# Denser steps of gated linear attention beside the last four projection tiles, the latents' scaling moved next to the last one, and five vector operations moved to GpSimd

## What is computed

```python
cq, ckv, kr, gq, gk, gv, gr, gg = jnp.split(x @ w_in, idx, axis=-1)
q = (rms_norm(cq, q_norm) @ w_uq).reshape(B, T, MLA_HEADS, MLA_NOPE + MLA_ROPE)
q_rope = apply_rope(q_rope, cos[:, None, :], sin[:, None, :])
k_rope = apply_rope(kr, cos, sin)
ckv = rms_norm(ckv, kv_norm)
...
o = o_intra + jnp.einsum('bhnid,bhndv->bhniv', q_t, S_prev)      # GLA, chunk by chunk
...
gla = rms_norm(gla_o.astype(dtype), gla_norm) * jax.nn.silu(gg.reshape(B, T, GLA_HEADS, GLA_DV))
mix = jnp.concatenate([mla, gla.reshape(B, T, GLA_WIDTH)], -1) @ w_out
```

## Time and profile before

| what | value |
|---|---|
| time of three runs, median | 1333.73 us (1331.41 to 1333.77) |
| the profiled execution's own time | 1331.96 us |
| its span in the trace | 1328.6 us |
| TensorE busy | 1248.8 us (94% of the span) |
| VectorE, ScalarE, GpSimd busy | 835.9, 561.2, 174.1 us |
| tiles 14 to 17 with slots 0 to 47, in the trace | about 240.4 to 342.0 us |
| end of that to the first attention scores | 342.0 to 397.4 us |

### The profile page before, as it was taken

How to read it: one execution, slowest core, us unless ns; L and a number is a source line. 1 busy time by engine, 2 the same in 40 slices (tenths; PEclk the granted TensorE clock), 3 DMA queues, 4 the chain that set the end, 5 groups by cost and what they waited for, 6 DMA issues and landing times. The chain is left out here.

```text
span 1328.6 us, 24499 instructions
## 1 busy us (share of the span) xinstructions
PE 1248.8 (94%) x9650; PEld 1179.7 (89%) x9650; DVE 835.9 (63%) x1324; ACT 561.2 (42%) x925; POOL 174.1 (13%) x217
## 2 busy tenths in 40 slices
PE   7999998999788997999999999999999999999896
PEld 7987777899667776899999999999999999999896
DVE  4122212344797776567897777777657666668877
ACT  4212223144644445543755445444473333333335
POOL 3524333110000000032100000000000000000752
PEclk9999999999899999999999999999999999999898
DMA  8749888333420012232336878768588555555003
GB/s 292 232 147 297 282 273 289 114 108 95 127 50 11 11 49 63 88 133 69 90 110 231 285 264 296 265 258 289 196 300 290 174 177 177 189 191 183 9 17 112
DMA packets 116536, 226.91 MB, mean 171 GB/s; under 512 B 13203, under 2 KB 60581, under 8 KB 114118
## 3 DMA queue, kind: packets, MB, share of 16 engines
q1 hardware_dynamic: 110278, 208.57, 46.1%
q0 software_dynamic: 6144, 16.79, 4.1%
HBM read 165.54 MB, written 58.73 MB: 169 GB/s over the span
## 5 line engine op out<-in xcount | busy, mean ns | idle before, releaser
L2775 PE MATMUL psum<-step_hid_hi,step_w_hi 128*128 128x258 f32 x784 | 160.3, 286 | 7.2 <-DVE y_sums L2826 3.6
L2775 PE MATMUL psum<-step_hid_hi,step_w_lo 128*128 128x258 f32 x784 | 159.2, 285 | 0.0
L2775 PE MATMUL psum<-step_hid_lo,step_w_hi 128*128 128x258 f32 x784 | 158.7, 284 | 0.0
L355 PE MATMUL psum<-xTh,win_hi 128*128 128x344 f32 (+1 forms) x432 | 148.2, 343 | 9.6 <-DVE xTl L408 9.5
L355 PE MATMUL psum<-xTh,win_lo 128*128 128x344 f32 (+1 forms) x432 | 139.8, 324 | 0.0
L355 PE MATMUL psum<-xTl,win_hi 128*128 128x344 f32 (+1 forms) x432 | 139.7, 323 | 0.0
L2775 PEld LDWEIGHTS psum<-step_hid_hi,step_w_hi 128*128 128x128 f32 x784 | 123.8, 193 | 7.7 <-issue 3.8
L2775 PEld LDWEIGHTS psum<-step_hid_hi,step_w_lo 128*128 128x128 f32 x784 | 122.8, 192 | 0.0
L2775 PEld LDWEIGHTS psum<-step_hid_lo,step_w_hi 128*128 128x128 f32 x784 | 122.5, 192 | 0.0
L2392 PE MATMUL psum<-x_t_hi,w_variant_hi 128*128 128x258 f32 x512 | 103.9, 284 | 5.3 <-DVE hid_variants L2509 2.9
L2737 ACT ACTIVATE step_hid_hi<-step_hid_raw 128x2064 fp32r<-128x2064 f32 x21 | 40.6, 1933 | 152.5 <-PE psum L2775 145.7
(11 more groups left out here) (409 smaller groups left out, 2999.9 us busy)
## 6 DMA issues: line engine op xcount, KB each, us to landing
step_hid_raw<-hid_rows SPq DMA_DIRECT2D x21, 1032.0 KB, 7.5
k_pages<-in_pages SPq DMA_DIRECT2D x128, 160.0 KB, 3.1
v_pages<-in_pages POOLq DMA_DIRECT2D x128, 128.0 KB, 4.4
w_raw<-in_w SPq DMA_DIRECT2D x16, 1024.0 KB, 5.1
hid_rows<-hid_variants SPq DMA_DIRECT2D x28, 516.0 KB, 3.3
step_w_raw<-w_sums SPq DMA_DIRECT2D x12, 1024.0 KB, 5.1
hid_rows<-hid_variants SPq DMA_DIRECT2D x14, 774.0 KB, 5.1
step_w_raw<-in_w SPq DMA_DIRECT2D x9, 1024.0 KB, 5.1
```

The source lines that it names most:

```text
L355: mm = pe.matmul(psum[0:M, 3 * (m % 2) + b, 0:BLK], w[:, m % 2, k, 0:M], x[:, k, b * BLK:(b + 1) * BLK], start=(k == 0 and i == 0), stop=( ...
L2775: mm = pe.matmul(slot(d)[:, s, :], wt[r][:, w], ht[r][:, TH * f + s * BW:TH * f + (s + 1) * BW], start=(f == 0 and i == 0), stop=(f == G - ...
```

## The change

The slots get a table of their own. `SLOT_AT` puts slot s behind product group 1 + 3s/2 (rounded down), that is after groups 1, 2, 4, 5, 7, 8 and so on, so 54 slots fit beside the four tiles, the last behind group 80 of 96. Weight splits and evacuations of gate tiles go to the first slot that comes late enough (`slot_after`). `pe_late` puts `gT` 0 behind group 88, `bc` 0 behind 92, `bc` 1 behind 94 and `gT` 1 behind 95. The other `gT` transposes are spread through the rotary query products. The SiLU of three gate tiles moves behind the last slots, and the last gate tile is evacuated between the splits of `cq`. Five vector operations of 1024 columns (two adds of squares, the three of the key's rotation) move from VectorE to GpSimd.

```diff
-                        if m >= ROW_GG and k % 2:
-                            pe_slot(pe, 12 * (m - ROW_GG) + 4 * b + k // 2)
+                        unit = 3 * KD * (m - ROW_GG) + KD * b + k
+                        if unit in SLOT_AT:
+                            pe_slot(pe, SLOT_AT[unit])
+                        if unit in LATE_AT:
+                            pe_late(pe, LATE_AT[unit])
...
-                   44: [("sO",)], 47: [("nk",)], 50: [("gT", 0), ("gT", 1)], 53: [("gT", t) for t in range(2, 5)]}
-        SLOTS = 12 * (NT - ROW_GG)
+                   44: [("sO",)], 47: [("nk",)]}
+        LATE_AT = {88: ("gT", 0), 92: ("bc", 0), 94: ("bc", 1), 95: ("gT", 1)}
+        SLOTS = 54
+        SLOT_AT = {1 + 3 * s // 2: s for s in range(SLOTS)}
...
         def act_gla(act):
-            for s in range(SLOTS, SLOTS + 6):
-                act_slot(act, s)
+            act_squares(act, 7)
+            act_root(act, 1)
             act.wait_ge(wr_loaded, WR_BASE + 64)
             hi_of(act, "wr")
+            act.wait_ge(proj_out, ROW_GG + 3)
+            act.activation(mixT[:, 4:7, :], mixT[:, 4:7, :], ACT.Silu).then_inc(silu_done, 1)
+            act.wait_ge(proj_mm, NT)
             act.wait_ge(cq_loaded, 16)
-            for k in range(3):
-                hi_of(act, f"cq{k}")
-            act_squares(act, 7)
-            act_root(act, 1)
+            hi_of(act, "cq0"), hi_of(act, "cq1")
+            act_evacuate_gg(act, 3)
+            hi_of(act, "cq2")
...
         def dve_gla(dve):
-            for s in range(SLOTS, SLOTS + 3):
-                dve_slot(dve, s)
             dve_rstd_rms(dve, 0)
             dve.sem_inc(rk_done, 1)
-            lo_of(dve, "wr"), lo_of(dve, "cq0")
-            for s in range(SLOTS + 3, SLOTS + 6):
-                dve_slot(dve, s)
-            lo_of(dve, "cq1"), lo_of(dve, "cq2")
-            gated(dve, 2), gated(dve, 3), gated(dve, 4)
             variance(dve, 1)
-            dve_ckv_scaled(dve, 0), dve_ckv_scaled(dve, 1)
+            lo_of(dve, "wr")
             rstd_gla(dve, 1)
             normed(dve, NORM_A, 8)
             dve.tensor_tensor(os_[:], os_[:], grs[:, 32:36].unsqueeze(2).broadcast_to([P, 4, DV]), ALU.mult).then_inc(osn_done, 1)
-            for t in range(NORM_A, 8):
+            dve_ckv_scaled(dve, 0), dve_ckv_scaled(dve, 1)
+            lo_of(dve, "cq0"), lo_of(dve, "cq1"), lo_of(dve, "cq2")
+            for t in range(8):
                 gated(dve, t)
...
         def pe_mla_in(pe):
+            pe_rope_in(pe, 0, 0)
+            pe_gla_task(pe, ("gT", 2))
             pe.wait_ge(proj_out, NT)
...
+            pe_rope_in(pe, 0, 1)
+            pe_gla_task(pe, ("gT", 3))
+            pe_gla_task(pe, ("gT", 4))
+            pe_rope_swap(pe, 0, 0)
+            pe_gla_task(pe, ("gT", 5))
+            pe_rope_swap(pe, 0, 1)
+            pe_gla_task(pe, ("gT", 6))
+            pe_gla_task(pe, ("gT", 7))
             pe_gla_task(pe, ("gTs",))
...
+        def pool_mla_in(pool):
+            for k in (1, 2):
+                pool.wait_ge(cqsq_done, k + 1)
+                pool.tensor_tensor(cqsq[:, 0], cqsq[:, 0], cqsq[:, k], ALU.add).then_inc(cqsum_done, 1)
+                pool.wait_ge(cqsum_done, k)
+            pool.wait_ge(kr_loaded, KR_BASE + 96)
+            pool.wait_ge(rope_loaded, ROPE_BASE + 32)
+            pool.tensor_tensor(krd[:], krd[:], rope[0], ALU.mult)
+            plink(pool, pool.tensor_tensor(krs[:], krs[:], rope[1], ALU.mult))
+            pool.tensor_tensor(krd[:], krd[:], krs[:], ALU.add).then_inc(kr_done, 1)
...
             lo_of(dve, "uv")
-            dve_krope(dve)
             dve.wait_ge(gst_stored, 80)
```

More of the change, by code:

```diff
@@ L1110, in dve_slot @@
                 ins.then_inc(gstate_done, 1)
-            if r == 3 and s % 12 == 3 and s // 12 < 3:
-                split_lo(dve, ROW_GG + s // 12 + 1)
+            for j in range(3):
+                if s == slot_after(j, 3):
+                    split_lo(dve, ROW_GG + j + 1)
             if r == 5 and 1 <= t <= 8:
@@ L1155, in dve_slot @@
                     dve_var_rms(dve, 0, gb, task, 2 * P)
-                elif task[0] == "gT" and task[1] < 2:
-                    gated(dve, task[1])
         def variance(dve, i):
@@ L1408, in pe_norm_sums, with pe_late @@
             return mm
[L1410 to L1419 removed]
+        def pe_late(pe, key):
+            if key[0] == "gT":
+                pe_gla_task(pe, key)
+                return
+            b = key[1]
+            mb.begin(pe, key)
+            pe.wait_ge(proj_out, NT - 1)
+            pe.wait_ge(rk_done, 1)
+            for j in range(4):
+                t = 4 * b + j
+                mm = pe.matmul(mb.of(key)[:, j * P:(j + 1) * P], rstdc[:, 0, t:t + 1].broadcast_to([P, P]), ident, start=True, stop=True)
+            mb.full(mm)
@@ new lines, in pe_rope_in, with pe_rope_swap @@
+        def pe_rope_in(pe, pr, b):
+            mb.begin(pe, ("qr", pr, b))
+            for k in range(3):
+                split(pe, f"cq{k}")
+                mm = passes(pe, mb.of(("qr", pr, b)), [((wrh[:, pr, k], wrl[:, pr, k]), (cqh[:, k, C2[b]], cql[:, k, C2[b]]))], start=(k == 0), stop=(k == 2))
+            mb.full(mm)
+        def pe_rope_swap(pe, pr, b):
+            mb.begin(pe, ("qs", pr, b))
+            pe.wait_ge(qx_done, 2 * pr + b + 1)
+            mb.full(pe.matmul(mb.of(("qs", pr, b)), const("swap"), xr[:, pr, C2[b]], start=True, stop=True))
@@ L1421, in pe_mla_in @@
         def pe_mla_in(pe):
+            pe_rope_in(pe, 0, 0)
+            pe_gla_task(pe, ("gT", 2))
             pe.wait_ge(proj_out, NT)
-            pe.wait_ge(rk_done, 1)
-            for b in range(2):
-                mb.begin(pe, ("bc", b))
-                for j in range(4):
-                    t = 4 * b + j
-                    mm = pe.matmul(mb.of(("bc", b))[:, j * P:(j + 1) * P], rstdc[:, 0, t:t + 1].broadcast_to([P, P]), ident, start=True, stop=True)
-                mb.full(mm)
-            split(pe, "cq2")
```

65 lines of the change are left out of this document (21 added, 44 removed).

## The result

The changed kernel takes 1338.5 us (median of 10 runs, 1333.7 to 1340.5); the kernel before, run beside it, 1331.6 (10 runs, 1330.6 to 1336.4). The ratio is 1.0044, 95% interval 1.0032 to 1.0057: slower by about 6 us (the two medians lie 6.9 apart). The forecast was 1332.7 with no measurable change, so it was wrong in value and in sign, and the time lies just outside its range. So this trace shows less than the usual loss; an execution of a usual length is read further down.

The account below looks back on a forecast made before the run. TensorE, busy 94% of the span, was taken as the bound, VectorE nearly so in the changed stretch. First scores came out -0.5 us, or -1.5; taking -1.0 from 1333.7 gave 1332.7 us, range 1328.3 to 1338.0.

Parts of the forecast that it names:

- What bounds the kernel now: Whole span and changed stretch: TensorE busy 94%, VectorE nearly the bound; waits and slow clock some 13 us to be had.
- Step 1: Projection tiles with denser slots: added work, group breaks and longer waits put the last product group's end at 349.4 us.
- T: End of the projection's last product group, forecast at 349.4 us; later times are counted from it.
- Step 2: Projection's end to rotary queries: TensorE waits about 3 us for `cq`, clock loss 1.0, second pair's products end at T+18.9.
- Step 3: GpSimd beside VectorE: VectorE loses 6.1 us of work, but contention adds 3.5; low parts of `ckv` at T+26.2.
- the term for contention: VectorE's two-SBUF-input operations beside GpSimd at 1.6 times their length, some 3.5 us; GpSimd at 40 to 60% speed.
- Step 4: From `nq` to first scores: TensorE waits 2.7 us for GpSimd's second add, first scores at 396.9 against 397.4.
- VectorE wins more: Rotation stretch: contention costs VectorE 1 us instead of 3.5; 3.5 to 5 us better, 1328 to 1329.5; chance 0.32.
- GpSimd's queue becomes the path: Key, last of five on GpSimd, delays first scores: 1337 to 1341 us; chance 0.16.
- its deciding point: The key's end on GpSimd at T+34.5, from which it would set the first scores.
- The slots cannot keep pace: Beside the projection tiles: denser slots wait, 4 us more and a lower clock, 1337 to 1338; chance 0.10.
- It does not do what it says: Early half microseconds are given back by waits for the same events: 1333.7, within the forecast's range, no chance of its own.

Follow-up runs that it names:

- e10: The changed kernel, unaltered, in one further profiled execution: 1334.3 us.
- e11: The changed kernel, unaltered, in another further profiled execution: 1339.8 us.
- e6: The changed kernel with the two adds back on VectorE and the key on GpSimd as soon as it is loaded: 1334.2 us, ratio 1.0015 to before.
- e9: The changed kernel, all five operations still on GpSimd, the key's three only after `wuv_lo`: 1331.4 us, ratio 1.0001 to before.
- e2: The changed kernel with all five operations back on VectorE, slots and late tiles as changed: 1327.9 us, ratio 0.9973 to before.
- e5: The changed kernel with each of GpSimd's five operations cut into four pieces of 256 columns: 1332.3 us, ratio 1.0003 to before.
- e12: The changed kernel with all five operations back on VectorE, repeated on another chip: 1330.7 us, ratio 0.9978 to before.

## Why the prediction was wrong, step by step

**What bounds the kernel now**: right. The waits of the earlier trace rows did go, and the stage stayed one where VectorE sets the pace.

**Step 1 (T = 349.4)**: held. The last product ends at 348.0 in the profiled execution. Its last matmul starts at 347.5 to 353.4 in the four; that the average is 349.4 is luck, since the spread comes from ahead of the changed code. From the first matmul on `gvT` to the end of the last product all four take 100.9 us, where the forecast had 101 (248.3 to 349.4). `gvT` waits 3.3 us (3.5 forecast) and the bank at slot 45 0.7. A wait for `w4` (+0.4) does not show.

**Step 2**: held. TensorE waits 2.67 us and twice a quarter for `cq_lo`, and the rotary products of the second pair are over at T+18. The clock did not fall there; in e10 and e11, the same code, it did, and cost 0.3 us to the first scores, so the 1.0 us for it was too much.

**Step 3 failed, in the term for contention.** I had put 3.5 us on VectorE and a rate of 40 to 60% on GpSimd. Measured are 7.2 us on VectorE and nearly full speed on GpSimd: 2.67 to 2.80 us an operation beside VectorE, 2.35 to 2.42 in the quietest cases (e6, e9). I had the adds over at T+21.6 to 23 and the key at T+32 to 33.5; they ended at T+17.3 and T+25.6. `ckv_lo` was there at T+28.5, not T+26.2. (Two of the sums behind these do not come out as written: T+22.5 and 3.5 us make T+26.0, and 13.5 us of work from T+12.5 to T+32 or 33.5 is a rate of 64 to 69%, not 40 to 60%.) The error was to turn one row, 2.00 us instead of 1.22 for a split of 1024 columns, into a ratio of 1.6 and apply it to operations of another length. It was not a rate but a wait for the rest of a running GpSimd operation, with the work of its own behind it. A wait does not shrink with the operation that has to wait; it is bounded by the length of the other engine's. An operation of 0.69 us that waits out the rest of a GpSimd operation of 2.4 to 2.8 becomes three to four times as long. The view that says so was there, in GpSimd's line for its first adds in the kernel before (operation, count, duration min/median/max in ns), and in VectorE's timeline beside them:

```profile
L425 POOL TENSOR_TENSOR x_T_raw<-x_T_raw x7: 2407/2421/3272, 21.1 to 36.9; 128x1032 f32<-128x1032 f32 x7
```

```profile
36.45 1.50 DVE L400 TENSOR_TENSOR win_lo<-win_raw,win_hi 128x1024 fp32r<-128x1024 f32 x1 [9.33 <-ACT win_hi L395]
```

The median add takes 2.42 and the slowest 3.27, later by most of a VectorE operation; I had used the mean (2.73). And the next split beside the adds takes 1.50, not 2.00: one length alone, two different waits. A shared rate would have given the same twice. The adds that were running when the two splits (25.11 and 36.45) began show it:

```profile
23.59 2.44 POOL L425 TENSOR_TENSOR x_T_raw<-x_T_raw 128x1032 f32<-128x1032 f32 x1
...
34.44 2.42 POOL L425 TENSOR_TENSOR x_T_raw<-x_T_raw 128x1032 f32<-128x1032 f32 x1
```

They end at 26.03 and 36.86, and the splits end at 27.11 and 37.95: 1.08 and 1.09 us later, each time. The add behind each took the 3.27 us.

**Step 4 failed with it.** The forecast wait of 2.7 us for GpSimd's sum in front of `nq` did not come, since GpSimd was early; instead TensorE waited 7.0 us for `ckv_lo`, which was in no rival, and its clock was 0.50 after it. From T to the first scores I had 47.5 us; it took 51.9 (52.2 from the last matmul's start, 52.0 to 52.5 in the four executions). The table load was hidden, as forecast. The arithmetic of that difference: against e2, whose stretch from the last matmul's start is 45.9, `ckv_lo` should end 7.2 - 2.5 = 4.7 us later (four waits, less the adds; the traces have 4.5), and nine of the queries' matmuls follow each other every 0.43 us instead of 0.23 at the low clock, 1.7 us. Together 6.4; 6.3 measured.

**The rivals.** *VectorE wins more* fell at the 7.2 us. *GpSimd's queue becomes the path* had the sign and the lock, but the wrong loser: GpSimd's key was there at T+25.6, nine microseconds before its deciding point. I had read "blocked for the whole instruction" as something that happens to the engine that joins a busy one. In these traces the two engines take turns by operation, and then the one with the shorter operations loses more of its time: VectorE lost 7.2 us of 12, GpSimd about 0.3 us an operation. With GpSimd in short pieces (e5) it was the other way round: VectorE lost 2.9 us up to `ckv_lo`, and GpSimd over its twenty pieces about 5 (19.9 less 20 x 0.73, an estimate). *The slots cannot keep pace*: no such wait, and e2 gains. *It does not do what it says*: it does.

**The chances.** Slower had 0.26, for two mechanisms of which neither came; the one that came was the blocking of the short operations on VectorE's path, which was priced inside the forecast, at half.

## What to carry to other kernels

Elementwise work with two SBUF inputs on GpSimd and on VectorE at the same time was exclusive here, operation by operation: price it as the number of VectorE's two-input operations that fall beside it times the rest of a GpSimd operation (here mostly 1.2 to 2.2 us each), not as a percentage. Before moving work to GpSimd, list what VectorE does in the stretch where it will run, and if short two-input operations there lie on the path, leave it, put it beside operations that read PSUM, or cut it into short pieces. A move that takes 6.1 us off the busiest engine of its stretch cost 0.65% by itself here; without it, the rest of the change (e2, 0.9973 and 0.9978) beats the changed kernel by far and the kernel before by a little.

## What the runs showed of the hardware

- A two-input operation of VectorE that waited for GpSimd came out mostly 1.2 to 2.2 us longer at GpSimd operations of 1024 columns and 0.3 to 0.5 us at 256; it ended 0.5 to 0.7 us after the GpSimd operation did where it takes 0.7 to 0.8 alone, and 1.08 where it takes 1.2 to 1.3; with one input in PSUM it never changed (0.68 to 0.69 in every kernel).
- GpSimd notices less: 2.67 to 2.86 us instead of 2.35 to 2.42 beside VectorE's operations of 0.7 us, and more beside its long ones (3.37 beside a `cq_lo` of 1.28 us, in e6). The same work in pieces of 256 columns takes it 19.9 us instead of 13.5.
- After the same wait, TensorE's granted clock fell in one execution of a kernel and not in another: behind the 2.3 us for `ckv_lo` it fell to 0.50 in e12 and stayed at 1.00 in e2. Over the stretch from the last product to the first scores it was 0.93 and 0.96, with 48.4 and 45.9 us.
- The wait of the paged attention for its `k_pages` transfers varied from 5.5 to 9.8 us between executions of one kernel, and moved everything behind it.
